# Eight-expert SwiGLU: from three split products on 128 rows to plain fp32 products on 32-column blocks

## The reference

```
def swiglu(h, w1, w3, w2):
    return (jax.nn.silu(h @ w1) * (h @ w3)) @ w2

def moe_swiglu(h, router, w1, w3, w2):
    logits = (x @ router).astype(jnp.float32)
    top_val, top_idx = lax.top_k(logits, TOP_K)        # TOP_K = 2 of 8
    gate = jax.nn.softmax(top_val, axis=-1).reshape(-1)
    ...
    yd = lax.map(lambda a: swiglu(a[0], w1[a[1]], w3[a[1]], w2[a[1]]), (blocks, blk_e))
    contrib = yd.reshape(-1, d)[dest] * gate[order][:, None]
    return jax.ops.segment_sum(contrib, tok[order], num_segments=n)
```

## Time and profile before

| | |
|---|---|
| median of 3 runs | 1670.03 us (1668.68 to 1672.45) |
| span of the profiled execution | 1673.7 us; no other time of it is given |
| PE busy | 1634.0 us, 98% |
| PEld busy | 1336.6 us, 80% |
| DVE busy | 1115.4 us, 67% |
| ACT busy | 843.8 us, 50% |
| moved | 424.43 MB, mean 254 GB/s |

### The profile page before, as it was taken

How to read it: one execution, slowest core, us unless ns; L and a number is a source line. 1 busy time by engine, 2 the same in 40 slices (tenths; PEclk the granted TensorE clock), 3 DMA queues, 4 the chain that set the end, 5 groups by cost and what they waited for, 6 DMA issues and landing times.

```text
span 1673.7 us, 23920 instructions
## 1 busy us (share of the span) xinstructions
PE 1634.0 (98%) x8908; PEld 1336.6 (80%) x8908; DVE 1115.4 (67%) x1336; ACT 843.8 (50%) x916; POOL 189.4 (11%) x242
## 2 busy tenths in 40 slices
PE   9999999999999999999999999999999999999997
PEld 6877776799999897777667788888888888888875
DVE  3554527366554374543627888888988888888987
ACT  3343422143343224442123677777767777777764
POOL 4221022100000333003213000000000000000020
PEclk8999999999999999999999999999999999999999
DMA  9649161835453775234284999999999999999993
GB/s 270 188 157 289 60 163 40 256 104 177 151 167 110 207 215 156 91 103 117 82 279 159 387 355 392 362 401 354 403 375 374 404 367 397 361 396 366 392 393 120
DMA packets 217988, 424.43 MB, mean 254 GB/s; under 512 B 18006, under 2 KB 113782, under 8 KB 217844
## 3 DMA queue, kind: packets, MB, share of 16 engines
q1 hardware_dynamic: 204592, 382.79, 64.5%
q0 software_dynamic: 12896, 40.29, 7.5%
q10 hardware_dynamic: 420, 0.28, 0.1%
HBM read 403.15 MB, written 24.29 MB: 255 GB/s over the span
## 4 chain that ended last, share of the span: by engine, by line
PE 88%; DVE 6%; DMA 2%; ACT 1%; DVEq 1%; issue 1%; ACTq 0%; SPq 0%
PE ps L763 84%; PE ps L767 4%; DVE arena L1890 2%; DMA weights_in<-in_moe_w 2%; ACT weights_high L1461 1%; DVE arena L2263 1%; ACT arena L1458 1%; DVEq L2128 1%; DVE weights_low L1890 1%; DMA arena<-in_const 0%; DVE arena L2129 0%; DVE arena L2266 0%; DVEq L2533 0%; ACT arena L1461 0%; DVE arena L2645 0%
## 5 line engine op out<-in xcount | busy, mean ns | idle before, releaser
L1890 DVE TENSOR_TENSOR weights_low<-weights_in,weights_high 128x3072 fp32r<-128x3072 f32 (+2 forms) x199 | 590.4, 2985 | 96.5 <-ACT weights_high L1461 95.9
L1461 ACT ACTIVATE weights_high<-weights_in 128x3072 fp32r<-128x3072 f32 (+2 forms) x199 | 490.4, 2477 | 188.9 <-PE ps L763 153.7
L763 PE MATMUL ps<-arena 128*128 128x288 f32 (+20 forms) x2832 | 525.7, 363 | 16.3 <-DVE arena L1890 9.6
L763 PEld LDWEIGHTS ps<-arena 128*128 128x128 f32 (+9 forms) x2832 | 374.5, 170 | 152.7 <-issue 49.9
L763 PE MATMUL ps<-weights_high,item_high 128*128 128x512 f32 x712 | 281.4, 395 | 2.1 <-DVE weights_low L1890 1.3
L763 PE MATMUL ps<-weights_high,item_low 128*128 128x512 f32 x712 | 277.8, 390 | 0.0
L763 PE MATMUL ps<-weights_low,item_high 128*128 128x512 f32 x712 | 277.6, 390 | 0.0
L763 PEld LDWEIGHTS ps<-weights_high,item_high 128*128 128x128 f32 x712 | 134.1, 188 | 30.2 <-DVE weights_low L1890 3.6
L763 PEld LDWEIGHTS ps<-weights_high,item_low 128*128 128x128 f32 x712 | 134.0, 188 | 28.5
L763 PEld LDWEIGHTS ps<-weights_low,item_high 128*128 128x128 f32 x712 | 134.2, 188 | 26.8
L1458 ACT ACTIVATE arena<-arena 128x128 f32<-128x128 f32 (+12 forms) x191 | 75.5, 409 | 140.5 <-DVE arena L1890 93.5
(11 more groups left out here) (210 smaller groups left out, 1837.0 us busy)
## 6 DMA issues: line engine op xcount, KB each, us to landing
weights_in<-in_moe_w SPq DMA_DIRECT2D x192, 768.0 KB, 8.7
weights_in<-in_moe_w SPq DMA_DIRECT2D x48, 1536.0 KB, 10.2
weights_in<-in_moe_w SPq DMA_DIRECT2D x64, 512.0 KB, 5.9
ffn_in<-in_ffn_w SPq DMA_DIRECT2D x30, 1024.0 KB, 7.2
weights_in<-in_moe_w SPq DMA_DIRECT2D x16, 1024.0 KB, 9.4
arena<-in_w_in SPq DMA_DIRECT2D x32, 384.0 KB, 3.9
token_slots<-arena SPq DMA_DIRECT2D x12, 512.0 KB, 7.8
arena<-in_w_out SPq DMA_DIRECT2D x16, 384.0 KB, 3.9
```

The lines of the kernel that those rows point to most:

```text
L763: return nc.tensor.matmul(out, lhsT, rhs, start=start, stop=stop)
L1461: return nc.scalar.activation(out, x, ACT.Copy, scale=scale)
L1890: return V.tensor_tensor(out, x, y, op)
```

## The change

An item has 96 rows (CAP) in three blocks of 32; up to 13 items, and a second item for an expert above 96 rows. There is no split in this stage: the raw unit is the moving operand of plain fp32 matmuls. Each of them has 32 stationary columns and writes 32 PSUM partitions. A chunk's w1 and w3 columns are cut into four pieces of n = 384 (or 256). Partitions 0 to 95 of banks 0, 1 and 2 get pieces 0, 2 and 3 of the three row blocks, and partitions 96 to 127 of the three banks get piece 1, one row block in each bank. So each group of four matmuls fills all four column groups. `down` does the same with the output halves of two hidden slices, in banks 5 to 7. Below, "quad" means four such matmuls.

Eight raw buffers replace six raw and three high ones; a transfer waits for the unit eight before. The functions `high` of ScalarE and `low` of VectorE and the splits of rows and gated values are gone. silu, `result` and the square buffers of ACT follow the new layout; VectorE turns gated rows and item rows by twelve 32x32-block transposes each, in place of TensorE's. ScalarE copies the turned rows from X0 (A0') to X1 (chunks 1 to 3).

```diff
-NITEM = 12
+CAP = 96
+NITEM = 13
-NRAW = 6
+NRAW = 8
-AHEAD = 6
+AHEAD = 8
...
# SyncE
+                    unit(0, "A", 1, 2, 6)
+                    unit(0, "A", 1, 3, 7)
...
-                            sp.wait_ge(used.sem, NB_U * w + u + 7)
+                            sp.wait_ge(used.sem, NB_U * w + u + 5)
...
# TensorE
-                    def product(o, xh, xl, wh, wlo, first, last):
-                        mm(o, xh, wh, first, False)
-                        mm(o, xh, wlo, False, False)
-                        return mm(o, xl, wh, False, last)
...
+                    def up(c, j, b, x):
+                        n = CHW[c] // 2
+                        w = raw[b][:, 0:8 * n].rearrange("p (k x n) -> p k x n", k=2, x=4)
                         for i in range(2):
                             k = 2 * j + i
+                            for bank, half in enumerate((0, 2, 3)):
+                                for t in range(3):
+                                    rows = slice(32 * t, 32 * t + 32)
+                                    mm(ps[rows, bank, 0:n], x[:, k, rows], w[:, i, half, :], k == 0, k == KD - 1)
+                                rows = slice(32 * bank, 32 * bank + 32)
+                                m = mm(ps[96:128, bank, 0:n], x[:, k, rows], w[:, i, 1, :], k == 0, k == KD - 1)
                         m.then_inc(used.sem, 1)
+                    def down(c, pair, b0, b1):
+                        n = CHW[c] // 256
+                        f = (2 * pair, 2 * pair + 1)
+                        w = [raw[(b0, b1)[x // n]][:, x % n * D:x % n * D + D] for x in f]
+                        first, last = c == 0 and pair == 0, c == 3 and pair == n - 1
+                        x = gT[c % 2]
+                        for bank, (i, half) in enumerate(((0, 0), (0, 1), (1, 0))):
+                            for t in range(3):
+                                rows = slice(32 * t, 32 * t + 32)
+                                mm(ps[rows, 5 + bank, :], x[:, f[i], rows], w[i][:, 512 * half:512 * half + 512], first, last)
+                            rows = slice(32 * bank, 32 * bank + 32)
+                            m = mm(ps[96:128, 5 + bank, :], x[:, f[1], rows], w[1][:, 512:1024], first, last)
...
+                            if kind == "A":
+                                if j == 0:
+                                    pe.wait_ge(m_g.sem, 4 * w + (c if c else 4))
+                                    if c == 0:
+                                        pe.wait_ge(x0_t.sem, w + 2)
+                                    elif c == 1:
+                                        pe.wait_ge(x1_a.sem, w + 1)
+                                pe.wait_ge(raw_in[b].sem, PER_ITEM[b] * w + landed(units, u))
+                                up(c, j, b, X1 if c else X0)
...
+                            if j == 0:
+                                pe.wait_ge(m_t.sem, 4 * w + c + 1)
...
# ScalarE
                     def silu(w, c, u):
                         act.wait_ge(used.sem, NB_U * w + LEAD + u + 9)
-                        fn(sl[:, 0:CHW[c]], ab_ps[:, 0:CHW[c]], ACT.Silu).then_inc(m_sil.sem, 1)
+                        n = CHW[c] // 2
+                        fn(sl[0:CAP, 0:n], ps[0:CAP, 0, 0:n], ACT.Silu)
+                        for t in range(3):
+                            e = fn(sl[32 * t:32 * t + 32, n:2 * n], ps[96:128, t, 0:n], ACT.Silu)
+                        e.then_inc(m_sil.sem, 1)
                     def result(w, u):
...
+                        copy(yS[0:CAP, 0:512], ps[0:CAP, 7, :]).then_inc(y_a.sem, 1)
+                        for t in range(3):
+                            e = copy(yS[32 * t:32 * t + 32, 512:1024], ps[96:128, 5 + t, :])
+                        e.then_inc(y_a.sem, 1)
...
# VectorE
                     def gated(k, c):
                         dve.wait_ge(m_sil.sem, k)
+                        tt(gm[0:CAP, 0:n], sl[0:CAP, 0:n], ps[0:CAP, 1, 0:n], ALU.mult)
+                        tt(gm[0:CAP, n:2 * n], sl[0:CAP, n:2 * n], ps[0:CAP, 2, 0:n], ALU.mult).then_inc(m_g.sem, 1)
+                        dve.drain()
+                        for t in range(3):
+                            for r in range(4):
+                                rows, part = slice(32 * t, 32 * t + 32), slice(32 * r, 32 * r + 32)
+                                i = V.transpose(gT[c % 2][part, 0:CHW[c] // P, rows],
+                                                gm[rows, 0:CHW[c]].rearrange("p (f x) -> p f x", x=P)[:, :, part])
+                        i.then_inc(m_t.sem, 1)
+                    def item_turned(w):
+                        dve.wait_ge(xin_in.sem, 16 * w + 16)
+                        dve.wait_ge(x1_a.sem, w + 1)
++                        for t in range(3):
+                            for r in range(4):
+                                rows, part = slice(32 * t, 32 * t + 32), slice(32 * r, 32 * r + 32)
+                                i = V.transpose(X0[part, :, rows], xin[rows, :].rearrange("p (k x) -> p k x", x=P)[:, :, part])
+                        i.then_inc(x0_t.sem, 1)
+                    def result(w, units):
+                        for half in range(2):
+                            dve.wait_ge(y_a.sem, 2 * w + half + 1)
+                            x = yS[0:CAP, 512 * half:512 * half + 512]
+                            i = tt(x, x, ps[0:CAP, 5 + half, :], ALU.add)
...
                     def item(w, units):
                         gated(4 * w + 2, 1)
...
+                            item_turned(w)
                         gated(4 * w + 3, 2)
...
                         gated(4 * w + 4, 3)
+                        if len(units) == NB_U:
+                            gated(4 * w + 5, 0)
...
+                        result(w, units)
# GpSimd
-                pool.wait_ge(x_pe.sem, w + 2)
-                pool.dma_start(xin, xi[w + 1]).then_inc(xin_in.sem, 16)
+                pool.wait_ge(x0_t.sem, w + 1)
+                pool.dma_start(xin[0:CAP, :], xi[w + 1]).then_inc(xin_in.sem, 16)
                 pool.wait_ge(yS_ev.sem, w + 2)
-                pool.dma_start(xi[w], yS).then_inc(yd_st.sem, 16)
+                pool.dma_start(xi[w], yS[0:CAP, :]).then_inc(yd_st.sem, 16)
```

More of the change, by code:

```diff
@@ L1383, in up @@
                         m.then_inc(used.sem, 1)
-                    def down(c, j, g, high=gTh, low=gTl):
+                    def down(c, pair, b0, b1):
                         n = CHW[c] // 256
-                        wh, wlo = (t[:, 0:n * D].rearrange("p (f d) -> p f d", f=n) for t in (Wh[g % 3], Wl[g % NRAW]))
-                        for i in range(n):
-                            f = n * j + i
-                            for b in range(2):
-                                x = slice(512 * b, 512 * b + 512)
-                                m = product(ps[:, 6 + b, :], high[:, f, :], low[:, f, :], wh[:, i, x], wlo[:, i, x],
-                                            c == 0 and f == 0, c == 3 and f == 2 * n - 1)
-                        m.then_inc(used.sem, 1)
@@ L1428, in item @@
-                            if kind == "C" and c < 3 and j == (0 if len(units) < NB_U and c == 2 else 1):
-                                turn_gated(w, c + 1)
+                            if j == 0:
+                                pe.wait_ge(m_t.sem, 4 * w + c + 1)
+                                if c == 0:
+                                    pe.wait_ge(yS_ev.sem, w + 1)
+                            pe.wait_ge(raw_in[b].sem, PER_ITEM[b] * w + landed(units, u))
+                            for pair in range(n // 2) if j == 0 else range(n // 2, n):
+                                down(c, pair, b if j == 0 else (b - 1) % NRAW, b if j else (b + 1) % NRAW)
@@ L1805, in item @@
                             act.wait_ge(glt_pe.sem, glt_pe.at(0))
-                            copy(GlT, ps[:, 5, 0:N]).then_inc(glt_a.sem, 1)
-                            high(w, units, 18)
-                            gated_high(w, 3, Xh)
-                            high(w, units, 19)
+                            copy(GlT[0:CAP, :], ps[0:CAP, 3, 0:N]).then_inc(glt_a.sem, 1)
                             fn(warm, c("eps"), ACT.Sqrt)
-                            act.wait_ge(used.sem, NB_U * w + LEAD + 19 + 9)
-                            act.wait_ge(y_free.sem, w + 1)
-                            copy(yS[:, 0:512], ps[:, 6, :]).then_inc(yl_a.sem, 1)
-                    act.sem_inc(yS_ev.sem, 1)
+                            result(w, 19)
                     act.sem_inc(y_free.sem, 1)
@@ L2351, in _ @@
                         rows_weighted_ffn(0)
-                    if l == 1 and d in (4, 6):
-                        dve.wait_ge(hi.sem, d // 2 - 1)
-                        lowest(d // 2 - 2, UW)
                 dve.drain()
@@ L2548, in low @@
[L2548 to L2556 removed]
+                        tt(Gl[:, 0:2, 0:CAP], Gl[:, 0:2, 0:CAP], Gr[:, 0:2, 0:CAP], ALU.add)
@@ L2571, in item @@
                     def item(w, units):
```

(10 more changed lines are left out.)

256 lines of the change are left out of this document (59 added, 197 removed).

## The result

The changed kernel takes 1643.12 us (median of 4 runs, 1641.61 to 1648.70); the kernel before took 1671.24 in the same session (1668.68 to 1675.48). The ratio is 0.9826, with a 95% interval of 0.9800 to 0.9853: 28 us faster. The forecast was 1625.4 with a range of 1604 to 1685, so the sign and the range held and 18 us of the forecast gain of 44.6 did not come. The profiled execution tells the same: a span of 1647.1 against 1673.7, 26.6 us less.

A forecast was written before the change was run, and what follows sets the result against it. PE was taken as the bound, with transfers close behind. Gains of 35.3 (seven periods), 9.1 (last item) and 1.4 (start), less 1.2 (end), make 44.6 us: span 1673.7 to 1629.1, time 1625.4 us, range 1604 to 1685.

The forecast's parts named there:

- 129 quads lose 3.9 us: Matmuls of an item: 0.03 us lost per quad, where 396 matmuls lost 5.4 us before; passes stay 84.48 us.
- overlap rival: Column groups overlap worse in a long stream: kernel at 1753 us, milder form 1718; chance 0.13.
- The period of 88.35: PE's time per item after the change, 5.05 us less than 93.40, counted for seven periods: 35.3 us gained.
- I take 404 as the rate of the engines when they always have work: DMA engines' rate in GB/s, from 4 us windows; an item's 35.39 MB in 88.35 us needs 401.
- Cost zero: Weight transfers: 275.0 MB left land at 1588 us, before PE wants the last unit at about 1610, so no loss.
- the trough: DMA rate falling to 239 GB/s with chunk 3's small units in flight; eight buffers were to remove it.
- transfer rival: Transfers become the bound at 382 GB/s: 275.0 MB take 720 us, kernel at 1642 us; chance 0.20.
- Late item rows: Rival: item rows reach VectorE late, PE stalls 16 us in each of seven items, 1737 us; chance 0.05.
- The last item: Stage's final item without A0': 72.3 us instead of 81.4, a gain of 9.1.
- Start and end: A1 starts at 922.1 instead of 923.48, gain 1.4 us; combining matmuls after C3 end later, loss 1.2 us.
- ScalarE and VectorE: Splitting work on both engines leaves, 16 us per four units; off the chain except at start and last item.

The follow-up runs named there:

- flat: Changed kernel with TensorE's loop over items written out, seven items and the last in a straight line: 1639.98 us, 0.9799 of the kernel before.
- pairs: Changed kernel with TensorE's loop body holding two items, two returns in place of six: 1640.44 us, 0.9817 of the kernel before.
- before_pairs: Kernel before the change with TensorE's loop body holding two items: 1685.7 us in one run, against 1672.0 of the kernel before.
- flat_gather128_again: Second run of flat with item 0's rows gathered at 128 columns per matmul instead of 96: 1634.15 us, 0.9774 of the kernel before.
- flat_long_rows: flat with chunk 3's A units filled with 4-KB rows of w2, same bytes, instead of 2-KB pieces: 1637.21 us, 0.9792 of the kernel before.
- blocks_of_96: Changed kernel with the three 32-column matmuls of a quad's A units merged into one of 96 stationary columns: 2285.43 us in one run.
- quarter: Changed kernel with a quarter of each weight unit's columns transferred after the first eight units: 1619.23 us in one run.

## Why the prediction was right, and where it was not

The direction and the range held, and part of that is luck. In the six periods the loop's return, for which the prediction has no term, cost 35.1 us (22.7 of gaps and 12.4 of slow clock), and the quads gave 18.1 more than forecast (6 x 3.0): two errors of opposite sign that leave the 17.0. The transfer rate, taken too high, would have kept the kernel at 1636 to 1640 even with the loop written out.

**The quads: right, and better than forecast.** "129 quads lose 3.9 us" is the step. They lose 85.33 - 84.48 = 0.85 us, below 0.01 each and not 0.03. The single quads of the earlier trace rows, with other matmuls on both sides, bounded the price from above; in a stream of quads it is near the lower bound of 0.00. The overlap rival is refuted. The Trainium skill (TensorE: Matmul & The Clock Gate, Part 3, "Measured speedup vs the span model") gives 2.38 for three column tiles, 0.79 of perfect. This case's trace does not agree: four blocks take 0.645 us where one after the other they would take 2.56, which is 3.97, or 0.99 of perfect.

**The period of 88.35: wrong by 2.8 us, in two terms with opposite signs.** The quads gave 3.0 more than forecast. The period is nonetheless 91.2 on average, by a step that the prediction does not have: TensorE's return to the start of a loop body grown from some 850 to 2064 matmul and load records, 3.8 us each, and 2.1 us a period of slow clock (five of the six periods have a return before them, the first has the wait for VectorE). The prediction put this term at nothing; flat, pairs and before_pairs show that it belongs to the return of a long body. The trace of before could not show it as a row, for its returns were free.

**Transfers: "I take 404 as the rate of the engines when they always have work", and "Cost zero".** This is the step that is wrong whatever the loop does. 404 is what quiet windows give; over whole items with every queue full (flat and its descendants) it is 391 to 392. The windows over two items (1193 to 1373.7 us) of flat_gather128_again read 395 with all other traffic in it. The 9 GB/s from 404 are 2.0 us per item; what else moves (395 against 391) is the rest of the 2.8 us between 87.6 and 90.4. The windows show two dips that come near the 2.0: 0.8 us after the item rows' fetch, and about 1.2 us for the small units of chunk 3 (in flat 324 and 363 GB/s for 4 us each). That they are the whole of it is not shown: in flat_long_rows the second dip was gone from its place and the period stayed. The prediction said that eight buffers remove the trough; they don't. In the changed kernel five windows from 1412 to 1432 us still read 300 to 363 at a share of 0.92 to 1.01, and in flat the low windows are at 0.90 and 1.02, so most of it isn't for want of work. The kernel before had a warning that was not read: over one whole item (1017.15 to 1110.55 us) its windows show 385 GB/s at a share of 1.00, so a share of 1.03 would be an estimated 397, not 404. The prediction named 391 as the rate below which the transfer sets the end, for a TensorE of 88.35 us per item; against 85.3 us, 391 is clearly a bound: 90.4 per item. The transfer rival had the right mechanism with too low a rate (382), and its 1642 us, so near to the 1643 measured, is not a confirmation: in the changed kernel TensorE waited for no transfer, and TensorE's returns set the time. Without them it would have been the transfer, at 1636 to 1640.

**Late item rows: rightly small.** Stores and fetches of item rows landed in 6.9 and 7.7 us (medians), and TensorE waited for VectorE once in the stage, 3.4 us at the start.

**The last item: a gain of 9.1, about right.** The seventh period and the last item together took 158.6 us, 2.0 less than forecast, though the seventh began at the slow clock. No landing is in the chain after 925 us, and the eight buffers are what does it: with six, two landings are in the chain there, and the same stretch takes 164.5 us (1471.77 to 1636.32).

**Start and end.** The gain of 1.4 us at the start became a loss of 1.5. The clock is low from before A0 begins until 908, and A0 starts 2.1 us later. The prediction kept the slow clock at its 1.45 us and did not ask what the shorter gather matmuls, part of the same change, do to it; with 128 columns the clock stayed at 1.00 in four profiles of four. What of the start's 2.9 us this accounts for is not shown in the times. At the end the loss is 1.6, not 1.2.

**ScalarE and VectorE** lost 461 and 437 us of work, as forecast. No run takes this apart from the rest; TensorE's waits show only VectorE's 3.4 us at the start.

## What to carry to other kernels

When an edit multiplies the instructions of a loop body, ask what the return costs: look for "issue" steps at the period of the loop in the chain and for the packets of the instruction queue; writing the loop out removed the wait here. When an engine gets faster, price the transfer by the mean over whole periods with full queues, not by the best windows, and treat a near tie as open: here both sides were mis-sized by some 3%, TensorE's period as well as the rate. Note the first refill: once transfers set the pace, the end of the kernel is that moment plus bytes over rate (731.7 to 732.1 us in three profiles).

## What the runs showed of the hardware that was not expected

- A TensorE loop body of some 850 matmul and load records (kernel before) and of some 1300 (blocks_of_96: 54 instruction packets in all) came back without a wait, and the packets show no reading; one of 1700 or 2064 was read anew, with a wait of 3.6 to 3.9 us per return in the changed kernel and of two stops of 2.3 to 3.3 us per return in before_pairs, beside full weight queues, and of 1.2 to 1.75 us beside a quarter of that traffic. Where between 1300 and 1700 the limit lies is open.
- Four plain fp32 products of 32 columns in four column groups: 0.645 us for 384 columns, 0.005 beyond their passes. A product of 96 columns beside one of 32: no overlap.
- A standstill of 3.6 to 3.9 us was followed by TensorE at 1.2 GHz (0.50) after five of six returns of the changed kernel, for 1.7 to 3.0 us of lost time each; 1.2 to 1.75 us in quarter did not.
- The gather before the stage: the granted clock fell in eight profiles of eight with 96 columns per matmul, in none of four with 128.
